# Attention in a transformer block: where the inverse roots of two norms are computed

## The reference

```python
q_a, k_a, v_a, q_b, k_b, v_b = _in_proj(h, w_in[l])
q_a = _axial_rope(_rms_norm(q_a, qn_a[l]), row_pos, col_pos)      # 8 heads of 64
q_b, k_b = _rms_norm(q_b, qn_b[l]), _rms_norm(k_b, kn_b[l])       # 8 heads of 64
o_a = _window_gqa_latent(q_a, k_a, v_a, k_ac, v_ac, sink_a[l])    # width 512
o_b = _neighbourhood_latent(q_b, k_b, v_b, k_bc, v_bc, rpb_b[l])  # width 512
x_new = x + g1 * _merge(o_a, o_b, on_a[l], on_b[l], w_out[l])

def _rms_norm(x, g):
    y = xf * lax.rsqrt(jnp.mean(xf * xf, axis=-1, keepdims=True) + EPS)   # EPS = 1e-6
    return (y * g).astype(x.dtype)

def _merge(o_a, o_b, g_a, g_b, w_out):
    return jnp.concatenate([_rms_norm(o_a, g_a), _rms_norm(o_b, g_b)], axis=-1) @ w_out
```

## Time and profile before

| | |
|---|---|
| time, median of 3 runs | 2662.96 us (2660.82 to 2667.11) |
| the profiled execution's own time | 2666.72 us |
| its span | 2664.9 us |
| TensorE busy | 2585.8 us, 97% |
| VectorE, ScalarE, GpSimd busy | 1474.3, 1041.7, 1149.5 us |
| chain that ended last | PE 81%, DVE 12%, issue 3%, ACT 3%, DMA 1% |
| the attention's loop | from about 322 us to about 660 us |

### The profile page before, as it was taken

The page is one execution under the profiler, slowest core; times in us unless marked ns, Lnnn a source line. Parts: engine busy times, 40 slices in busy tenths (PEclk is TensorE's granted clock), DMA queues, the critical chain, the costliest instruction groups (busy, mean ns, idle before and its releaser), DMA issues.

```text
span 2664.9 us, 33072 instructions
## 1 busy us (share of the span) xinstructions
PE 2585.8 (97%) x12561; PEld 2092.1 (79%) x12561; DVE 1474.3 (55%) x1880; ACT 1041.7 (39%) x1715; POOL 1149.5 (43%) x689
## 2 busy tenths in 40 slices
PE   7999999899999999999999999999998999999997
PEld 5778799898878888888886777667877888887885
DVE  5672289898267655654334111224179788876333
ACT  4551477788254333221113441224244444441113
POOL 0233223563375555555444211113465555555452
PEclk8999999999999999999999999999999999999998
DMA  7462101223312322233322111001511222235321
GB/s 286 145 197 62 36 28 27 65 77 100 116 56 88 104 86 87 87 124 129 100 76 102 40 32 40 24 25 34 172 48 65 78 94 81 72 110 194 99 79 63
DMA packets 71581, 235.12 MB, mean 88 GB/s; under 512 B 8945, under 2 KB 11121, under 8 KB 71298
## 3 DMA queue, kind: packets, MB, share of 16 engines
q1 hardware_dynamic: 71426, 233.02, 26.7%
HBM read 179.77 MB, written 39.85 MB: 82 GB/s over the span
## 4 chain that ended last, share of the span: by engine, by line
PE 81%; DVE 12%; issue 3%; ACT 3%; DMA 1%; POOL 0%; SPq 0%; DVEq 0%; ACTq 0%
PE S L863 17%; PE S L463 11%; PE S L464 11%; PE S L841 9%; PE S L845 9%; PE S L842 9%; PE S L697 2%; PE M L948 2%; PE M L713 1%; DVE pt L1708 1%; DVE S L1689 1%; DVE xt L1804 1%; PE M L466 1%; PE S L681 1%; PE S L963 1%
## 5 line engine op out<-in xcount | busy, mean ns | idle before, releaser
L2186 POOL TENSOR_TENSOR wbl<-rf,wbh 128x512 fp32r<-128x512 f32 (+1 forms) x352 | 512.9, 1463 | 478.4 <-ACT wbh L1256 478.2
L1256 ACT ACTIVATE wbh<-rf 128x512 fp32r<-128x512 f32 (+1 forms) x352 | 215.0, 620 | 691.2 <-PE S L863 360.6
L2063 POOL TENSOR_TENSOR wl<-raw,wh 128x1024 fp32r<-128x1024 f32 x59 | 147.4, 2500 | 573.9 <-ACT wh L1018 573.9
L841 PE MATMUL S<-th_t,wbh 128*128 128x512 f32 x640 | 253.0, 395 | 6.4 <-POOL wbl L2186 3.6
L845 PE MATMUL S<-tl_t,wbh 128*128 128x512 f32 x640 | 252.3, 394 | 0.0
L842 PE MATMUL S<-th_t,wbl 128*128 128x512 f32 x640 | 251.7, 393 | 0.0
L863 PE MATMUL S<-fh,wbh 128*128 128x512 f32 x704 | 221.1, 393 | 2.6 <-DVE xt L1756 2.6
L863 PE MATMUL S<-fl,wbh 128*128 128x512 f32 x704 | 220.0, 392 | 1.3 <-POOL fl L2210 1.3
L863 PE MATMUL S<-fh,wbl 128*128 128x512 f32 x704 | 220.1, 392 | 0.0
L463 PE MATMUL S<-hh,wh 128*128 128x512 f32 (+1 forms) x456 | 194.2, 426 | 10.5 <-DVE gt L1992 3.1
L841 PE MATMUL S<-th_b,wbh 128*128 128x512 f32 x480 | 189.3, 394 | 0.7 <-ACT ub L1361 0.4
(11 more groups left out here) (347 smaller groups left out, 5795.9 us busy)
## 6 DMA issues: line engine op xcount, KB each, us to landing
ff<-hid SPq DMA_DIRECT2D x44, 512.0 KB, 6.2
rf<-in_w_d SPq DMA_DIRECT2D x80, 256.0 KB, 2.7
mr<-in_w_modT SPq DMA_DIRECT2D x32, 512.0 KB, 5.1
rf<-in_w_f1g SPq DMA_DIRECT2D x22, 512.0 KB, 3.7
rf<-in_w_f1u SPq DMA_DIRECT2D x22, 512.0 KB, 3.5
hid<-pr SPq DMA_DIRECT2D x22, 512.0 KB, 2.6
rf<-in_w_f2g SPq DMA_DIRECT2D x22, 512.0 KB, 5.3
rf<-in_w_f2u SPq DMA_DIRECT2D x22, 512.0 KB, 3.6
```

The source lines that it names most:

```text
L841: e.matmul(o, hi[:, k, :], th[part][:, k, :], start=k == 0, stop=False)
L1256: e.activation(flat(wbh[wslot(f, n)][:, :, :])[:, 0:x.shape[1]], x, ACT.Copy).then_inc(*w_hi.mark((f, n)))
L2063: e.tensor_tensor(l, raw[:, w % 3, 0:n], h.bitcast(F), ALU.subtract).then_inc(*w_lo.mark(w))
L2186: e.tensor_tensor(l, x, h.bitcast(F), ALU.subtract).then_inc(*w_lo.mark((f, n)))
```

## The change

The four activations of i = 78 are taken out of ScalarE's program. GpSimd gets a function `root` of two instructions: a multiplication and an addition (scale, then 1e-6), and a power with the exponent -0.5, which is read from a new column of `mv`. At i = 12 it makes the root of `rsl` (128 x 1024), at i = 79 the one of the eight sums in `oss` (128 x 8). The multiplications of o_a now read `oss`, and VectorE's scaling of unit 17 waits for GpSimd's root. The roots of the second half of the output (`out_ln(1)`, `out_exp(1)`) stay on ScalarE.

```diff
--- before.py
+++ after.py
@@ -24,7 +24,7 @@
 V_N2, V_MIX, V_FFN, V_FIN, V_GLN, V_CW, V_CB = 68, 76, 84, 92, 100, 108, 240
 V_N = 288
 
-M_MOD, M_CMOD, M_G1, M_GC, M_QA, M_QB, M_G2, M_KB, M_RAW = 0, 48, 64, 72, 80, 81, 82, 90, 96
+M_MOD, M_CMOD, M_G1, M_GC, M_QA, M_QB, M_G2, M_KB, M_POW, M_RAW = 0, 48, 64, 72, 80, 81, 82, 90, 91, 96
 M_N = 144
 
 NPM = 8
@@ -1175,13 +1175,6 @@
                                  ACT.Copy).then_inc(*a_out.mark(i - 5))
                 if 70 <= i < 78:
                     out_square(0, i - 70, (7, 1) if i == 70 else None)
-                if i == 78:
-                    out_ln(0)
-                    e.wait_ge(*a_ln(NU - 1))
-                    e.activation(rsl[:, :], rsl[:, :], ACT.Ln, bias=EPS).then_inc(*a_ln.mark("last"))
-                    out_exp(0)
-                    e.wait_ge(*a_ln("last"))
-                    e.activation(rsl[:, :], rsl[:, :], ACT.Exp, scale=-0.5).then_inc(*a_rs.mark(NU - 1))
                 if i == NI + 1:
                     split_hi(FIRST["out"])
                     for b in range(4):
@@ -1590,7 +1583,7 @@
                     g = vec[:, V_KA:V_KA + 1] if rope else vec[:, V_KB:V_KB + 1]
                 else:
                     g = mv[:, M_QA:M_QA + 1] if rope else mv[:, M_QB:M_QB + 1]
-                e.wait_ge(*a_rs(u))
+                e.wait_ge(*(p_osc("rs") if u == NU - 1 else a_rs(u)))
                 e.wait_ge(*d_ev(u))
                 if kind == "k" and not rope:
 
@@ -2128,8 +2121,22 @@
                 e.wait_ge(*p_v(("h", n)))
                 e.tensor_tensor(l_, v, h_.bitcast(F), ALU.subtract).then_inc(*p_v.mark(n))
 
+            def root(x, n, scale, event):
+
+                e.tensor_scalar(x, x, scale, 1e-6, ALU.mult, ALU.add).then_inc(*p_osc.mark((event, 0)))
+                e.wait_ge(*p_osc((event, 0)))
+                e.tensor_tensor(x, x, mv[:, M_POW:M_POW + 1].to_broadcast([128, n]), ALU.pow).then_inc(*p_osc.mark(event))
+
+            e.memset(mv[:, M_POW:M_POW + 1], -0.5).then_inc(*p_osc.mark("half"))
+            e.wait_ge(*p_osc("half"))
             head_in(1)
             for i in range(NI + 5):
+                if i == 12:
+                    e.wait_ge(*a_ln(NU - 1))
+                    root(rsl[:, :], 1024, 1.0, "rs")
+                if i == 79:
+                    e.wait_ge(*a_osq(("sq", 7)))
+                    root(oss[:, 0:8], 8, 1.0 / 512, ("r", 0))
                 if i >= 5:
                     n, kind, h, p, b, k0, L = ITEMS[i - 5]
                     if b % 4 == 3:
@@ -2148,8 +2155,8 @@
                 if i % 4 == 3 and 79 <= i < 111:
                     b = (i - 79) // 4
                     if b == 0:
-                        e.wait_ge(*a_osq(("r", 0)))
-                    e.tensor_scalar(oa[:, b, :], oa[:, b, :], ors[:, b:b + 1], None, ALU.mult).then_inc(*p_osc.mark((0, b)))
+                        e.wait_ge(*p_osc(("r", 0)))
+                    e.tensor_scalar(oa[:, b, :], oa[:, b, :], oss[:, b:b + 1], None, ALU.mult).then_inc(*p_osc.mark((0, b)))
                 if i == NI:
                     split_lo(FIRST["out"])
```

## The result

The changed kernel takes 2800.5 us (median of 4 runs, 2799.2 to 2802.6) against 2661.9 us for the kernel before on the same chip, a ratio of 1.0522 with a 95% interval of 1.051 to 1.0534. That is 5% slower, and 98 us above the upper end of the predicted range. The profiled execution of the changed kernel took 2800.2 us.

What follows compares the result with a forecast made beforehand. The attention loop was taken as bound by items passing between engines, so one engine's stop stops the others. 19.2 + 2 - 6.5 - 3 = +11.7 us on 2663.0 gave 2675 us, range 2654 to 2703 us.

Steps and rivals of the forecast that it cites:

- The gain: Items 78 to 82: ScalarE's stop and a second stop just behind it shrink, 9.5 us together, 5 to 12.
- ScalarE's stop: Item 78: table load and four activations hold ScalarE 5.0 us; removing them and the low clock gives -6.5 us (-5.0 to -7).
- the scaling of unit 17: VectorE, item 82: falls earlier in GpSimd's key preparation, most likely in the short cast; -3 us, between 0 and -5.
- The small root and the memset: GpSimd, item 79 and ahead of the loop: cost nothing; for the root an upper bound of a microsecond or two.
- The power's duration: GpSimd, item 12, 128x1024: 25 us assumed from 10 to 20 arithmetic steps a column, ends 2.4 and about 55 us.
- Rival (c): Item 12: the power is very long, over 55 us, same mechanism, 2705 us and up; chance 0.13.
- P: Duration of GpSimd's large power at item 12, taken as 25 us; the forecast median is 2663 + P - 13.3 above 6 us.
- Who waits: Behind the power at item 12: GpSimd can afford it for a while; VectorE's addition stands 19.2 us, then ScalarE and TensorE.
- VectorE's block: The addition of den and dsn at 362.31 us stands until GpSimd's power ends: 19.2 us, plus 2 us for the low clock.
- rival (d): The power doesn't hold VectorE; only head 3, for item 24, is late, 8.4 us: 2664 us at P = 25; chance 0.09.
- The rule on the shared port: VectorE instruction with two SBUF inputs and GpSimd instruction reading SBUF exclude each other, the later blocked throughout: 19.2 us stall.
- The estimate by the GPSIMD Engine Reference: Large power at item 12: 40 operations at 1.2 GHz over 1024 columns give 11 us, with the sum above 2661 us.

## Why the prediction was wrong

- **The gain: right in its mechanism.** ScalarE's stop and its low clock went (-6.5 us), and the scaling of unit 17 came earlier in GpSimd's work and met only the last 0.8 us of a step (forecast -3, about -4 in the loop). It was the subtraction for the queries, though, and not the cast of the keys. The whole gain was forecast as 9.5 us; the kernel without the large root shows 7.0, interval 4.5 to 9.3, so the forecast lies just above it, and 10.8 in the loop.
- **The small root and the memset: right.** 1.64 us, hidden; the next multiplication starts in time.
- **The power's duration: the step that failed.** "If a power is 10 to 20 such steps, that is 23 to 45 us" was arithmetic on a wrong price and a guessed count. The price of a step, 2.2 ns a column, came from a pass whose factor is read from SBUF; the scaling pass with two immediate factors takes 1.06 us for 1024 columns, no more than a copy, and not the 3.1 us that I took. The number of steps was no reading at all. The result was off by a factor of 6.5: 163.27 us in place of 25, and 55 as an upper end that no row bounded. Rival (c), over 55 us, had 0.13. This step makes the whole miss and a little more: with P = 163.3 the prediction's own sum, 2663 + P - 13.3, gives 2813 us, and the 12.5 us from there back to 2800.5 belong to the next point.
- **Who waits: right that both do, wrong which one counts.** The sum put VectorE's block, from 362.3 us to the power's end, as the term of P. VectorE was held, but for 73.7 of 154 us, and taking this away changed nothing. The term that set the time was that of rival (d), which I had kept for the case that VectorE is not held: head 3's queries in GpSimd's own queue. That rival's own numbers, 2664 us at P = 25, give 2664 + 138.3 = 2802 us for P = 163.3, against 2800.5 measured. The runs put the loss at P less about 20 us. A wait that lies inside a longer one on another path adds nothing; I added the shorter one and left out the longer.
- **The rule on the shared port: its condition holds, its extent does not.** The 73.7 us show that a VectorE instruction with two operands in SBUF is held by GpSimd, as the Trainium skill says (SBUF — State Buffer, section Who interferes with whom), and the form with a scalar operand is not. But "fully blocks until the first finishes" (the same page of the Trainium skill, section Summary: rules for kernel authors) is not what the power shows: it lets VectorE through 8.6 us after its start with up to 512 columns, and after 82 us of 163 with 1024. The short scaling passes agree with that sentence: they hold the addition to their end.
- **The estimate by the GPSIMD Engine Reference** (section 3.1 of that page of the Trainium skill, about 3 operations a cycle), 11 us with 40 operations, missed as well. Its rate may hold; the number of operations was mine there too.
- **The direction was right by luck.** A power of the 25 us that I assumed would, by the room of 20 us, have cost about 5 us and the gain been 7: no change, in place of the +11.7 us of my sum. That is an estimate from the runs, for a power that does not hold VectorE longer than head 3 is late; no run has that length, the nearest being the 20.76 us one, which cost nothing. The kernel came out slower because the power is far longer than I took it to be.

## What to carry to other kernels

An operation that no row shows has no upper end: before a wide one is moved to another engine, measure it at two small widths. Here 8 and 128 columns (1.64 and 20.76 us) give 0.159 us a column and 163 us for 1024; the eight alone, taken in proportion, would have said 210 us, already far from 25. What stands behind it in its own queue counts first: from the moment at which the queue's next product is needed follows how long the operation may be (20 us here), and waits on other paths that lie inside that one cost nothing. And where two table loads stop a tight loop, look for a place where the pipeline is still filling: the same two loads and activations cost 6.5 us at item 78 and about 1 us at most at item 0.

## What the runs showed of the hardware

- GpSimd's power, exponent -0.5: 0.16 us for each column of 128 float32 values and about 0.4 us besides (1.64, 20.76, 81.96, 122.68 and 163.27 us for 8, 128, 512, 768 and 1024 columns). A multiplication of the same operands takes 1.90 us for 1024.
- A VectorE addition of 128x4 with both operands in SBUF was held by a running power only where that had more than 512 columns, and then until 82 us after its start (436.57 - 354.62 and 437.06 - 354.69 us); additions that came later, beside the same power, were not held. The scaling pass ahead of the power held it to its end at every width from 128 to 1024 columns. With one tensor operand and a scalar from SBUF it was not held by the power (0.58 us for four).
- GpSimd's scaling by two immediates takes 1.06 us for 1024 columns, and its scaling by a factor from SBUF 1.57 us for 512.
